# Attention between two scans: the transposes of a query tile one turn later

## The chip, the core and the metric

The kernel runs on one core of a Trainium2 chip. The metric is the time on the device in microseconds (us). TensorE (PE) multiplies and transposes into PSUM, VectorE (DVE), ScalarE (ACT) and GpSimd (POOL) do the elementwise work, SyncE (SP) issues loads. Each engine works through its own list of instructions in the order in which it was written; semaphores tie the lists together. TensorE's clock is granted at one of two levels, 2.4 and 1.2 GHz, which the views show as 1.00 and 0.50.

## What is computed

Two transformer blocks over 1024 tokens of width 1024, one behind the other. The first has a mixing layer of two branches, latent attention and an RWKV recurrence that runs forward and backward, then a convolved feed-forward; the second has gated linear attention, a convolution and a feed-forward. The change touches the first block's attention, which is computed while the two RWKV scans run:

```python
def one_block(args):                        # 128 queries, 8 heads
    qn_b, qr_b = args
    s = (jnp.einsum('bqhd,bkhd->bhqk', qn_b, k_nope)
         + jnp.einsum('bqhd,bkd->bhqk', qr_b, k_rope))
    p = jax.nn.softmax(s.astype(jnp.float32) * scale, axis=-1)
    return jnp.einsum('bhqk,bkhd->bqhd', p.astype(v.dtype), v)
...
def step(state, inp):                       # one RWKV step, both directions
    r_t, w_t, k_t, v_t, a_t, b_t = inp
    sa = jnp.einsum('bhvk,bhk->bhv', state, a_t)
    state = (state * w_t[:, :, None, :] + sa[..., None] * b_t[:, :, None, :]
             + v_t[..., None] * k_t[:, :, None, :])
    return state, jnp.einsum('bhvk,bhk->bhv', state, r_t)
```

## The kernel before

The whole program is written as one list per engine. The stage that matters here is `scans` (line 1894). On every engine it holds four Python generators: `s0` and `s1` are the forward and the backward scan (`scan_pe`, `scan_ve`, `scan_ae`, `scan_ge`, `scan_sp`), `mid` is work between them, and `at_` is the attention. `interleave` (line 163) takes one step of each in the order s0, mid, s1, at_, again and again; one such round is called a turn. After seven turns of s0 alone s1 joins. A scan takes 28 steps for each of 8 chunks of 128 tokens (one step of 225 is the start), and each step is short: matmuls of 64 rows, which ScalarE or VectorE takes out of PSUM, and the scan's next step needs them.

The attention has 64 tiles, each 128 queries by 1024 keys of one head. Its steps for all engines come from one generator, `att_steps` (line 1101), to which each engine gives its own functions:

- `scores(i)`: on TensorE six matmuls of 512 columns into the two banks of `SIDE` (only one tile's scores fit there); on VectorE, as a part of `at_`, the maximum of each row (line 389) and its factor (line 382);
- `later(i)`: on ScalarE the exponential (line 1245), which writes one of two buffers `APB[i % 2]` and releases the score banks;
- `transp(i)`: on VectorE, as `mid` (`att_scale_ve`, line 1214), the reciprocal of the row sum (line 1218) and the scale of the probabilities (line 382, tile `HT`); on TensorE eight 128x128 transposes (line 372) into two banks of the ring `MAIN`, which the scans use too (six banks, taken in order); on ScalarE two copies of 128x512 out of these banks;
- `pv(m)`: on TensorE the product of the values and two tiles' probabilities, on ScalarE a copy, and for every fourth m two stores by GpSimd;
- `load(i)` on SP and `pieces` on ScalarE and GpSimd bring in keys and queries and split them in two parts.

Before the change a tile i has two turns. In the first all engines do `load(i)`, pieces, `scores(i)` and then `transp(i - 1)`; in the second `later(i)` alone, which is nothing on TensorE and VectorE. Behind an odd tile comes a third turn with `pv`. The exponential of tile i reads the maximum of tile i; the scale of tile i-1 reads the exponential of tile i-1; the transposes wait for the scale; the scores of tile i+1 wait for the exponential of tile i, since they take its banks. In a turn, VectorE's order is: step of s0, scale of tile i-1 (`mid`), step of s1, maximum of tile i (`at_`). TensorE's is: step of s0, step of s1, scores of tile i, transposes of tile i-1.

Of the kernel before, what the change touches and what calls it, by code (L numbers as in the profile page):

```python
# [235 lines left out]
def program(nc, a, out):  # L236
    ctx = ExitStack()
    with ctx:
# [862 lines left out]
        def att_steps(scores, transp, pv, load, later=lambda i: None, pieces=lambda *what: None):  # L1101
            load(-1)
            for _ in range(LEAD - 2):
                yield
            for c in range(4):
                pieces("k", 0, c)
            yield
            for c in range(2):
                pieces("q", 0, c)
            yield  # L1110
            for i in range(66):
                if i < 64:
                    load(i)
                    for kind, ahead, c in PIECES[i % 8]:
                        n = (i // 8 if kind == "k" else i // 8 * 2) + ahead
                        if n < (8 if kind == "k" else 16):
                            pieces(kind, n, c)
                    scores(i)
                if 1 <= i <= 64:
                    transp(i - 1)  # L1120
                yield
                if i < 64:
                    later(i)
                    yield
                if i % 2 and i >= 3:
                    pv((i - 3) // 2)
                    yield
# [14 lines left out]
        def att_turns(e):  # L1142
            return att_steps(skip, skip, skip, skip)

        def att_sp(sp):
# [17 lines left out]
            def load(i):  # L1163
# [10 lines left out]
                if i % 8 == 4 and i < 56:  # L1174
                    values(i // 8 + 1)
                    queries(i // 4 + 1)
            return att_steps(skip, skip, skip, load)

        def att_pe(pe):
# [23 lines left out]
            def pv(m):  # L1203
# [4 lines left out]
                for j in range(8):  # L1208
                    for y, cols_ in enumerate(ROWS):
                        x = mm(pe, ps[cols_, b, 0:P], AVH[h % 2][:, j, :], apt(2 * m + y)[:, j * P:(j + 1) * P], j == 0, j == 7)  # L1210
                x.then_inc(*pe.sig("pe_att", "pv", m))
            return att_steps(scores, transp, pv, skip)

        def att_scale_ve(ve):
# [2595 lines left out]
```

How the kernel before makes its waits and increments, by code:

```python
    def wait_ge(self, sem, value):  # L133
        if sem is not None and self.seen.get(id(sem), 0) < value:
            self.seen[id(sem)] = value
            self.e.wait_ge(sem, value)
# [197 lines left out]
        def take(pe, *key, n=1, banks=BANKS):  # L334
            b = plan.next_place(banks, key, n)[1]
            for tok in plan.releases(key):
                pe.wait_ge(*tok)
            return b
# [15 lines left out]
        def load_w(sp, src, *key, n=1024):  # L355
            i = plan.next_place(RING, ("w",) + key)[1]
            for tok in plan.releases(("w",) + key):
                sp.wait_ge(*tok)
            sp.e.dma_start(W[:, 1024 * i:1024 * i + n], src).then_inc(*dma(f"dma_w{i}", *key))
# [58 lines left out]
        def norm1_pe(pe):  # L418
            pe.wait_ge(*at("dma_cst", "all"))
            for t in range(NT + 1):
                if t == NT:
                    project(pe, t - 1)
                    break
                for h in range(2):
                    b = take(pe, "norm1", t, h)
                    pe.wait_ge(*at("ve_norm1", "xs", t))
                    for j in range(4):
                        i = tr(pe, ps[:, b, j * P:(j + 1) * P], TN[t % 2][:, (4 * h + j) * P:(4 * h + j + 1) * P])
                    i.then_inc(*pe.sig("pe_norm1", t, h))
                if t:
                    project(pe, t - 1)
# [1 line left out]
        def project(pe, t):  # L433
# [2 lines left out]
            o, ts_ = ps[:, b, 0:416], slice(t * P, (t + 1) * P)  # L436
            for g in range(2):
                pe.wait_ge(*at("ae_norm1", "hi", t, g))
                pe.wait_ge(*at("ae_norm1", "wm", g))
```

## Time and profile before

| | us |
|---|---|
| median of 3 runs | 3271.42 |
| lowest and highest | 3266.91, 3272.53 |
| the profiled execution | 3270.7 |
| its span, first to last instruction | 3268.9 |
| TensorE matmuls busy, of the span | 3151.0 (96%) |
| VectorE, ScalarE, GpSimd busy | 2089.2, 1296.5, 891.2 |
| mean granted clock of TensorE | 0.989 |

The profile is one execution. Its page names the engines' busy time; the views of the trace behind it show stretches of the span, groups of instructions, waits with what ended them, and instructions in order of time. Times in these views are counted from the first instruction. Weight loads have a row of their own (PEld) and lie beside the matmuls. The ends of matmuls are modelled, so that the next group's start can lie a little ahead of the end shown. A float32 matmul stands as two instructions.

### The profile page before, as it was taken

How to read it: one execution, taken by the hardware profiler on the slowest of the kernel's cores; microseconds unless marked ns; L12 is line 12 of the kernel's file. 1: busy time of each engine (PE TensorE's matmuls, PEld its weight loads, DVE VectorE, ACT ScalarE, POOL GpSimd, SP SyncE). 2: the span in 40 equal slices, each digit the busy share in tenths (PEclk: the TensorE clock that was granted, in tenths of full speed). 3: DMA queues.
4: the chain of work that ended last, by engine and by line, in shares of the span. 5: the costliest groups of instructions: out<-in, count | busy, mean ns of one | idle time of the engine just before them, and what ended most of it. 6: DMA issues, size and time to landing. Idle time of an engine off the chain costs nothing.

```text
span 3268.9 us, 61761 instructions
## 1 busy us (share of the span) xinstructions
PE 3151.0 (96%) x26560; PEld 2539.1 (78%) x26560; DVE 2089.2 (64%) x3031; ACT 1296.5 (40%) x2289; POOL 891.2 (27%) x778
## 2 busy tenths in 40 slices
PE   8989998999999988999999999999999999999998
PEld 8678777788888776467888888878677878888887
DVE  5363465666766665847899887762455475565686
ACT  4333334555555432124333344443333343333444
POOL 1232243232222222100577740000000026666100
PEclk9999999999999999999999999999999999999999
DMA  4251245111211221632132247522102322322753
GB/s 151 68 160 46 71 172 167 41 45 61 71 56 44 79 82 46 214 126 91 71 114 108 97 157 246 167 92 92 39 27 80 130 84 90 116 100 97 265 160 116
DMA packets 128016, 346.46 MB, mean 106 GB/s; under 512 B 15792, under 2 KB 19520, under 8 KB 124928
## 3 DMA queue, kind: packets, MB, share of 16 engines
q1 hardware_dynamic: 106592, 258.09, 24.0%
q0 software_dynamic: 21152, 84.42, 6.9%
q8 instruction: 210, 3.44, 0.5%
q14 instruction: 62, 0.51, 0.1%
HBM read 246.51 MB, written 95.94 MB: 105 GB/s over the span
## 4 chain that ended last, share of the span: by engine, by line
PE 85%; DVE 8%; ACT 4%; issue 2%; DMA 1%; POOL 1%; SPq 0%; DVEq 0%; ACTq 0%; POOLq 0%
PE ps L369 43%; PE ps L368 39%; PE ps L372 4%; DVE AR L378 2%; DVE X L378 2%; DVE SM L389 1%; DVE WS L378 1%; DVE W L378 1%; ACT AR L375 1%; DVE HT L382 1%; ACT WS L375 0%; ACT W L2226 0%; ACT X L375 0%; ACT HT L1245 0%; POOL AR L378 0%
## 5 line engine op out<-in xcount | busy, mean ns | idle before, releaser
L378 DVE TENSOR_TENSOR WS<-W,WS 128x512 fp32r<-128x512 f32 (+1 forms) x284 | 342.1, 1205 | 250.2 <-ACT WS L375 250.0
L368 PE MATMUL ps<-HH,WS 128*128 128x512 f32 x1280 | 394.3, 390 | 0.0
L368 PE MATMUL ps<-TO,WS 128*128 128x512 f32 x1440 | 346.0, 390 | 0.0
L375 ACT ACTIVATE WS<-W 128x512 fp32r<-128x512 f32 (+1 forms) x284 | 210.0, 739 | 315.5 <-PE ps L369 170.8
L368 PEld LDWEIGHTS ps<-TO,WS 128*128 128x128 f32 x1440 | 270.5, 188 | 55.9
L368 PEld LDWEIGHTS ps<-HH,WS 128*128 128x128 f32 x1280 | 240.4, 188 | 49.7
L368 PE MATMUL ps<-HL,WS 128*128 128x512 f32 x640 | 249.3, 390 | 0.0
L368 PE MATMUL ps<-TO 128*128 128x512 f32 x936 | 227.0, 390 | 0.2 <-DVE TO L378 0.2
L369 PE MATMUL ps<-AR 64*64 64x64 f32 (+2 forms) x5440 | 205.2, 244 | 22.3 <-ACT AR L375 11.0
L368 PE MATMUL ps<-WS 128*128 128x512 f32 x888 | 215.2, 390 | 0.1
L375 ACT ACTIVATE X<-ps 128x512 f32<-128x512 f32 (+1 forms) x168 | 100.3, 597 | 285.3 <-PE ps L369 129.1
L369 PE MATMUL ps<-HL,HI 128*128 128x512 f32 (+1 forms) x512 | 207.9, 406 | 2.8 <-POOL WL L378 2.8
L369 PE MATMUL ps<-WS,HH 128*128 128x512 f32 x640 | 203.2, 393 | 4.4 <-DVE X L378 1.5
L369 PE MATMUL ps<-WS,HL 128*128 128x512 f32 x576 | 206.5, 392 | 0.7 <-DVE X L378 0.7
L369 PE MATMUL ps<-HH,WS 128*128 128x512 f32 (+1 forms) x672 | 205.7, 395 | 1.2 <-ACT HH L375 1.2
L369 PE MATMUL ps<-HH,HI 128*128 128x512 f32 (+1 forms) x512 | 204.7, 400 | 0.0
L369 PE MATMUL ps<-HH,WL 128*128 128x512 f32 (+1 forms) x512 | 204.5, 399 | 0.0
L368 PEld LDWEIGHTS ps<-TO 128*128 128x128 f32 x936 | 175.2, 188 | 37.3 <-DVE TO L378 1.3
L369 PEld LDWEIGHTS ps<-AR 64*64 64x64 f32 (+1 forms) x5440 | 158.5, 138 | 56.3 <-issue 27.4
L368 PEld LDWEIGHTS ps<-WS 128*128 128x128 f32 x888 | 166.4, 188 | 34.7 <-DVE WS L378 0.5
L378 POOL TENSOR_TENSOR X<-X 128x1024 f32<-128x1024 f32 (+1 forms) x44 | 104.8, 2385 | 296.3 <-DVE X L378 225.3
L375 ACT ACTIVATE AR<-ps 128x512 f32<-128x512 f32 (+4 forms) x240 | 124.2, 522 | 153.8 <-PE ps L369 105.2
(367 smaller groups left out, 6417.7 us busy)
## 6 DMA issues: line engine op xcount, KB each, us to landing
AR_b<-h_d SPq DMA_DIRECT2D x154, 256.0 KB, 2.9
AR<-rw_d SPq DMA_DIRECT2D x104, 256.0 KB, 4.2
W<-in_w_fg SPq DMA_DIRECT2D x44, 512.0 KB, 3.9
W<-in_w_fu SPq DMA_DIRECT2D x44, 512.0 KB, 5.0
h_d<-FST POOLq DMA_DIRECT2D x20, 1024.0 KB, 4.4
x_d<-X POOLq DMA_DIRECT2D x24, 512.0 KB, 4.6
W<-in_w_tok SPq DMA_DIRECT2D x24, 512.0 KB, 4.4
rw_d<-X POOLq DMA_DIRECT2D x40, 256.0 KB, 3.4
```

What stands on the lines that cost most here:

```text
L368: return pe.e.matmul(o, l, r, start=start, stop=stop, skip_group_check=True)
L369: return pe.e.matmul(o, l, r, start=start, stop=stop)
L372: return pe.e.transpose(o, i, ident)
L375: return e.e.activation(o, x, ACT.Copy)
L378: return e.e.tensor_tensor(o, x, y, op)
L382: return e.e.tensor_scalar(o, x, s1, None, o1)
L389: return e.e.tensor_reduce(o, x, AX.X, op)
```

## The change

In `att_steps` the call of `transp(i - 1)` moves behind `later(i)`, and the `yield` that ends a turn now stands between `scores(i)` and the two. So the first turn of tile i has `load(i)`, pieces and `scores(i)`, the second `later(i)` and then `transp(i - 1)`. Tile 64 and 65, which have no scores, keep one turn each. All engines take the same generator, so the order changes on all of them at once.

```diff
                         if n < (8 if kind == "k" else 16):
                             pieces(kind, n, c)
                     scores(i)
+                    yield
+                if i < 64:
+                    later(i)
                 if 1 <= i <= 64:
                     transp(i - 1)
                 yield
-                if i < 64:
-                    later(i)
-                    yield
                 if i % 2 and i >= 3:
                     pv((i - 3) // 2)
                     yield
```

## Rows read from the trace of the kernel before

**Rows 1.** busy us by stretch: from:to, length, PE, PEld, DVE, ACT, POOL, clock, DMA

```profile
540.00:1124.00 584.00, 550.92 (x11709) 468.15 (x11707) 395.80 (x759) 306.74 (x661) 154.90 (x184) 0.99 0.19 57
1124.00:1290.00 166.00, 144.97 (x4025) 124.01 (x4024) 101.27 (x211) 57.33 (x128) 39.97 (x46) 0.96 0.21 70
1600.00:1700.00 100.00, 100.00 (x443) 82.88 (x442) 93.16 (x76) 39.33 (x67) 68.05 (x43) 1.00 0.29 103
```

**Rows 2.** waits of TensorE's matmuls, 540 to 1124: us, times, longest

```profile
PE ps L372 <- DVE HT L382: 8.7, 9, 2.2
...
PE ps L369 <- ACT HT L1245: 3.5, 4, 2.0
```

**Rows 3.** order of time, TensorE: start, us, engine, line, tiles, shape, count

```profile
807.67 1.65 PE L369 MATMUL ps<-KF,QF 96*128 96x512 f32 x6
809.16 1.04 PE L372 MATMUL ps<-CS,HT 128*128 128x128 f32 x8
810.13 1.08 PE L369 MATMUL ps<-AR 64*64 64x64 f32 x29
...
812.99 0.62 PE L369 MATMUL ps<-EX,AR 64*64 64x64 f32 x13
...
814.25 1.66 PE L369 MATMUL ps<-KF,QF 96*128 96x512 f32 x6
815.75 1.04 PE L372 MATMUL ps<-CS,HT 128*128 128x128 f32 x8
816.72 0.45 PE L369 MATMUL ps<-EX,AR 64*64 64x64 f32 x8
...
819.21 0.45 PE L369 MATMUL ps<-EX,AR 64*64 64x64 f32 x8
...
821.87 1.97 PE L369 MATMUL ps<-W,HT 128*64 128x128 f32 x32
```

**Rows 4.** order of time, VectorE, 809 to 819; brackets: idle before it, releaser

```profile
809.36 1.23 DVE L389 TENSOR_REDUCE SM<-ps 128x1 f32<-128x1024 f32 x1 [3.54 <-PE ps L369]
...
811.33 0.69 DVE L378 TENSOR_TENSOR EX<-ps,AR 128x512 f32<-128x512 f32 x1 [0.55 <-PE ps L369]
...
814.23 0.16 DVE L1218 RECIPROCAL SM<-SM 128x1 f32<-128x1 f32 x1 [0.51 <-ACT HT L1245]
814.43 0.75 DVE L382 TENSOR_SCALAR HT<-HT,SM 128x1024 f32<-128x1024 f32 x1
...
815.95 1.23 DVE L389 TENSOR_REDUCE SM<-ps 128x1 f32<-128x1024 f32 x1
...
817.68 1.51 DVE L378 TENSOR_TENSOR EX<-ps,EX 64x128 f32<-64x128 f32 x4 [0.32 <-PE ps L369]
```

**Rows 5.** waits of the weight loads, 540 to 1124, first and last of 17

```profile
PEld ps L369 <- issue: 40.1, 145, 1.4
...
PEld ps L369 <- DVE X L1644: 0.2, 1, 0.2
```

**Rows 6.** groups by line, 540 to 1124: count, busy us, mean ns, idle

```profile
L389 DVE TENSOR_REDUCE SM<-ps 128x1 f32<-128x1024 f32 x64 | 78.1, 1220 | 27.8 <-PE ps L369 27.1
L1245 ACT ACTIVATE HT<-ps,SM 128x1024 f32<-128x1024 f32 x64 | 71.0, 1110 | 0.0
...
L382 DVE TENSOR_SCALAR HT<-HT,SM 128x1024 f32<-128x1024 f32 x64 | 58.0, 906 | 2.3
...
L382 DVE TENSOR_SCALAR SM<-SM 128x1 f32<-128x1 f32 (+1 forms) x74 | 11.6, 156 | 2.5
```

**Rows 7.** order of time, ScalarE: the two copies of one tile's transposes

```profile
809.80 1.08 ACT L375 ACTIVATE W<-ps 128x512 f32<-128x512 f32 x2 [1.01 <-PE ps L372]
```

**Rows 8.** order of time, TensorE: transposes behind a long wait

```profile
735.69 1.06 PE L372 MATMUL ps<-CS,HT 128*128 128x128 f32 x8 [2.19 <-DVE HT L382]
```

**Rows 9.** busy time before and behind it, columns as in the first group

```profile
730.00:736.60 6.60, 4.41 (x55) 3.60 (x54) 6.06 (x8) 2.11 (x6) 4.23 (x4) 1.00 0.11 40
736.60:740.00 3.40, 3.40 (x56) 3.07 (x56) 2.11 (x4) 1.88 (x5) 0.07 (x1) 0.50 0.02 5
```

## Prediction

> **What bounds the kernel now.** The change touches only the stage in which the two RWKV scans and the attention run in turns, so I read by stage. The busy time of the engines in three stretches [rows 1] comes first: in 540 to 1124 us, where the attention runs, TensorE's matmuls are busy 550.92 of 584 us, VectorE 395.80 and ScalarE 306.74; 33.1 us are TensorE's own idle time, and that is about what there is to win. The waits of TensorE name the pieces of it [rows 2]: transposes that wait for the scaled probabilities (VectorE, line 382) 8.7 us, scores that wait for the exponential which frees their banks 3.5 us; the rest is spread over small waits, most of them of scan steps. In this stage TensorE is the bound, with VectorE next to it.
>
> The order of one turn is what the change turns on, so the third view is the order in time of two tiles, TensorE's instructions [rows 3] and VectorE's [rows 4]. I call the turn with the scores of tile i A, the one behind it B, and the turn with the product by the values, behind every odd tile's B, C. Turn A of tile 30 ends with scores (807.67) and transposes (809.16); B is the stretch 810.13 to 812.99 in which TensorE does scan work alone; A of tile 31 follows with scores at 814.25 and transposes at 815.75, its B from 816.72 to 819.21. VectorE reads in its own fixed order: maximum of tile 30 (809.36) and its scaling by a constant, the first scan's step of B (811.33), the second scan's, then in the next A the reciprocal and the scale of the probabilities (814.23, 814.43), then the next maximum at 815.95, right behind the scores' end.
>
> **The change, part by part.** No instruction is added or taken away and no turn: both orders have 64 A, 64 B, 2 closing A and 32 C turns, 162 in all. Three things move from A(i) to B(i), for 64 tiles: eight transposes on TensorE, the reciprocal and scale of tile i-1 on VectorE, two copies of 128x512 on ScalarE. SP and POOL execute none of the moved steps, and the loads, the pieces and their order against the scans stay; no DMA is issued by a moved step. On ScalarE the exponential of tile i now stands ahead of the copies of tile i-1.
>
> What it removes. The transposes no longer wait in A for a scale that itself waited for the exponential of the turn just before, and the empty turn B, in which a scan step follows the same scan's last one with only one other step between, gets 0.97 us of cover (809.16 to 810.13). The least this gives back is the two waits of attention itself, 8.7 + 3.5 = 12 us [rows 2]. The most is all idle time of the weight loads that has a releaser or none in the table: 17 rows that add up to 81.5 us, of which [rows 5] shows the first and the last. That is far too much, because a load also stands still while the array works on. I take 40 us: the 33.1 us of matmul idle, of which some stays, and some 0.1 us at each of the many waits that a pipelined matmul's modelled end hides.
>
> What it adds: a wait. Today the transposes of tile i-1 are covered twice: VectorE scales before the maximum of tile i is asked for, and TensorE has the scores (1.49 us from start to next start, 807.67 to 809.16) between the scan steps and the transposes. Behind the change VectorE reaches the scale only behind the maximum of tile i, which can't begin before the scores' end, and behind the first scan's step of B; and TensorE has only the two scan steps of B before it wants the transposes. In numbers, from the moment at which TensorE is through with the scores and would start B:
> - maximum and its factor: start 0.1, then 1.22 + 0.156 = 1.38 us [rows 6], so done at about 1.5;
> - the first scan's step on VectorE: the 395.80 us of VectorE less 64 times (1.22 + 0.906 + 2 x 0.156 = 2.44), or 156, leave 240 us for 320 steps (162 turns of one scan, 158 of the other), 0.75 us a step; and it waits for its own inputs, 0.55 us in B(30), 0.32 in B(31) [rows 4], nothing in the turns where that scan has no step for VectorE; I take 0.15 on the mean;
> - reciprocal and scale: 0.156 + 0.906 = 1.06 us [rows 6], and 0.06, an estimate, to the waiting transpose.
>
> That is 3.5 us. TensorE's two scan steps of B took 2.86 us in B(30) and 2.49 in B(31) [rows 3]. Their mean: 584 us less 33 idle, 64 x (1.49 + 0.97) = 157 and 32 x 1.9 = 61 for C's product (a group of 32 matmuls is 1.97 us long in [rows 3], and the next one begins some 0.07 before such an end) leave 333 us in 162 turns, 2.05 us; B turns hold the idle of their own too, so 2.2. The wait is 3.5 - 2.2 = 1.3 on the mean, and 64 of them are 80 us. Two turns by their own rows: B(30): 1.5 + 0.69 + 1.12 = 3.3 against 2.86, a wait of 0.4. B(31): VectorE begins the step at 1.5 instead of 0.96 and is 1.51 long, so 1.5 + 1.5 + 1.1 = 4.1 against 2.49, a wait of 1.6. As bounds for all 64 these give 26 to 102 us. Queued behind the waiting transposes on TensorE is everything, both scans' next steps; behind the scale on VectorE is the second scan's step of B, which TensorE wants only after the transposes (0.97) and one scan step (1.0), so 2.0 us later: it is covered.
>
> On ScalarE turn B now has the exponential, 1.11 us, and two copies, 1.08 us together [rows 6, 7]. The copies follow the transposes, which are late anyway; the next work behind them is the first scan's copy of the next turn, which TensorE needs a further turn later. I cost it at nothing; if the cover is gone it is at most 0.6 us in 64 turns, 38 us, and then the scans wait. The copies also free the two banks of the transposes for the ring of six; same cover.
>
> The clock. In 730.00:736.60 the granted clock is 1.00, TensorE waits 2.19 us for a scale (to 735.69), and from 736.60 the clock is 0.50, the lower level, for 3.4 us [rows 8, 9]. A repeated wait of 1 to 2 us can bring more of these. The stretch behind the attention, 1124 to 1290, is busy to 87% (144.97 of 166) and had 0.96 where the attention's stretch, 94% busy, had 0.99 [rows 1]. With 550.92 busy us in 584 + 40 the stage would be 88% busy; 0.03 less clock is 6% of the time at half rate, which stretches 551 us of work by 3%, 17 us if nothing covers it. Half of such time falls on waits; I take 5 us, bounds 0 and 17. The page "TensorE: Matmul & The Clock Gate" of the Trainium skill (Part 1) says the default state is throttled and activity releases the throttle; the 2.19 us wait and the fall behind it agree.
>
> Sum: +80 for the new wait, -40 for waits given back, +5 for the clock: +45 us. The profiled execution took 3270.7 us, its span 3268.9; it lies within 0.7 us of the median of 3271.4. So 3316 us.
>
> One rule bears on how much idle time there is. The Trainium skill, "Perfetto Trace Analysis", section "Identifying the Most-Contended Engine", says that matmul busy time is a poor measure and that the busy share of LDWEIGHTS is the one to use. By it, with the 82.88% of the stretch 1600 to 1700 as full, the 468.15 us of the attention's stretch are 565 us of full work [rows 1], so that 19 us could be won instead of 40 and the sum would be +66; the two stretches have matmuls of different sizes, so I keep to the matmuls' own idle time.
>
> **Rivals.** (a) The transposes fill the empty turn and their wait stays short: faster. This is what happens if VectorE reaches the scale in time, that is if the mean wait in B is under 40/64 = 0.6 us. For it: B(30) is such a turn, and VectorE is busy only 68% of the stage. Against it: the maximum follows the scores by 0.03 us today (809.32 to 809.36), so it can't come earlier, and no work stands between it and the transposes but two scan steps. With a mean of 0.3 us, 19 us, the time is -40 + 19 = -21: 3250 us. (b) The new wait takes just what it gives back, a mean of 0.6 us, or a larger give-back of 80: 3271 us. (c) The wait as forecast and the clock low for much of the stage, with ScalarE's double load not covered: +80 - 40 + 17 + 25 = +82, 3353 us.
>
> **How the numbers follow.** Forecast 0.62, with 3290 to 3335 of its own (wait 60 to 95, given back 30 to 50); (c) and all beyond 3335: 0.20; (b) 0.07; (a) 0.11. About 0.2% is what a measurement of this kernel can tell from no change. Slower by more holds the forecast and (c): 0.82; same 0.07; faster 0.11. The range goes from 3268, which leaves out (a), to 3360.
>
> **What the profile would show.** Right: the transposes' wait for line 382 grows from 8.7 to some 60 to 90 us and stands at the end of every B; the waits for line 1245 and the scan steps' waits shrink; VectorE runs maximum, one scan step, reciprocal and scale without a gap; the stage ends some 45 us later, at about 1170, and the rest is as long as before. Wrong: the transposes start right behind the second scan's step; or TensorE's scan steps wait for ScalarE's copies behind the exponential; or the granted clock of the stage falls below 0.95, which would put the time over 3335.

## The result and the profile after

The changed kernel takes 3362.1 us (median of 4 runs, 3359.44 to 3365.67) against 3269.64 us before in the same comparison, a ratio of 1.0283 with a 95% interval of 1.0266 to 1.0301. It is 92 us slower. The forecast was slower by 45 us, 3316 us, with a range that ended at 3360: the sign and the main mechanism (a new wait for the scale) held, the size was half of what came, and the time lies 2 us beyond the range.

In the two profiled executions, which differ by 91.8 us, nearly all of it is in the stage that the change touches. Busy time by stretch (from:to, length, then PE, PEld, DVE, ACT, POOL with their counts, granted clock, DMA share, GB/s), first of the kernel before, from its first scores to its last product by the values, and from there to the end:

```profile
538.60:1127.90 589.30, 556.22 (x11792) 472.61 (x11794) 398.84 (x766) 307.60 (x662) 158.32 (x188) 0.99 0.19 57
1127.90:3268.90 2141.00, 2082.11 (x12409) 1661.02 (x12408) 1427.64 (x1924) 794.52 (x1346) 579.59 (x441) 0.99 0.34 117
```

and the same two stretches of the changed kernel:

```profile
541.00:1219.40 678.40, 577.04 (x11792) 482.71 (x11794) 397.15 (x766) 310.57 (x662) 155.48 (x188) 0.96 0.16 50
1219.40:3360.60 2141.20, 2081.83 (x12408) 1659.46 (x12408) 1443.36 (x1924) 793.63 (x1346) 579.05 (x441) 0.99 0.33 117
```

Behind the stage the kernel is as long as before, to 0.2 us, and ahead of it 2.4 us longer (first scores at 541.0 instead of 538.6, in code that the change leaves alone). The stage is 678.4 - 589.3 = 89.1 us longer. TensorE has the same 11792 instructions; its idle time goes from 589.3 - 556.2 = 33.1 to 678.4 - 577.0 = 101.4 us, 68.3 more, and its busy time grows by 20.8 us, while the granted clock of the stretch falls from 0.99 to 0.96. The waits of TensorE's matmuls in the changed kernel (us in total, times, longest) say what the idle time is:

```profile
PE ps L372 <- DVE HT L382: 94.8, 61, 3.3
...
PE ps L369 <- ACT X L1723: 3.4, 3, 1.2
```

The transposes' wait for the scaled probabilities was 8.7 us in 9 places [rows 2] and is 94.8 in 61 now; the scores' wait for the exponential (3.5 us before) is gone from the list, and all waits for ScalarE together are 5.4 us. One tile in order of time, tile 31, whose turn A and B are in [rows 3, 4]. TensorE first, then VectorE:

```profile
849.83 1.66 PE L369 MATMUL ps<-KF,QF 96*128 96x512 f32 x6
851.42 0.45 PE L369 MATMUL ps<-EX,AR 64*64 64x64 f32 x8
...
852.17 1.97 PE L369 MATMUL ps<-X 64*64 64x64 f32 x48
855.38 1.06 PE L372 MATMUL ps<-CS,HT 128*128 128x128 f32 x8 [1.25 <-DVE HT L382]
856.38 0.45 PE L369 MATMUL ps<-EX,AR 64*64 64x64 f32 x8
```

```profile
851.52 1.23 DVE L389 TENSOR_REDUCE SM<-ps 128x1 f32<-128x1024 f32 x1 [0.80 <-PE ps L369]
852.78 0.15 DVE L382 TENSOR_SCALAR SM<-SM 128x1 f32<-128x1 f32 x1
852.86 1.51 DVE L378 TENSOR_TENSOR EX<-ps,EX 64x128 f32<-64x128 f32 x4
854.30 0.14 DVE L1218 RECIPROCAL SM<-SM 128x1 f32<-128x1 f32 x1
854.48 0.75 DVE L382 TENSOR_SCALAR HT<-HT,SM 128x1024 f32<-128x1024 f32 x1
```

TensorE is through with the scores at 851.42 and with both scan steps at about 854.1. VectorE begins the maximum when the scores are done and then works without a gap: maximum, factor, the four instructions of the first scan's step, reciprocal, scale. The transposes start 0.15 us behind the scale, 3.96 us behind the start of the turn. The prediction had put 4.1 us there for this tile. The Trainium skill ("TensorE: Matmul & The Clock Gate", the section on the array's architecture) says that ScalarE and VectorE are strict first-in-first-out; these rows agree.

The clock, columns as in the first view: a stretch in which the transposes wait for a scale, and the one behind it.

```profile
866.00:869.90 3.90, 1.54 (x30) 1.22 (x26) 2.65 (x7) 1.97 (x4) 0.00 (x0) 1.00 0.00 0
869.90:873.30 3.40, 3.40 (x66) 3.28 (x64) 0.57 (x2) 0.71 (x2) 0.00 (x0) 0.51 0.03 5
```

The eight transposes in it waited 2.36 us and began at 868.45; then the clock is at its lower level for 3.4 us. From 546 us to the stage's end there are 14 stretches at the lower level, 55 us together, where the kernel before had two, 10 us. Each of the 14 begins in a wait of TensorE of 1.7 to 3.3 us or at most 1.5 us behind one, and both of the two began so, at waits of 2.2 us. 18 more waits of 1.5 us and over brought no such stretch.

### The profile page after: what moved, and what is told of

It is laid out like the page before. It is cut to its first block, busy times and chain, and to the rows that moved or that the text cites. A ratio compares the mean times of both kernels' runs of the same rounds, so it can differ in the third digit from the quotient of the medians.

```text
span 3360.6 us, 61759 instructions
## 1 busy us (share of the span) xinstructions
PE 3174.1 (94%) x26560; PEld 2547.9 (76%) x26560; DVE 2103.3 (63%) x3031; ACT 1298.6 (39%) x2289; POOL 887.8 (26%) x778
## 4 chain that ended last, share of the span: by engine, by line
PE 83%; DVE 11%; ACT 3%; issue 1%; DMA 1%; POOL 0%; SPq 0%; DVEq 0%; ACTq 0%; POOLq 0%
PE ps L369 41%; PE ps L368 38%; PE ps L372 4%; DVE SM L389 2%; DVE AR L378 2%; DVE HT L382 2%; DVE X L378 1%; DVE W L378 1%; DVE WS L378 1%; DVE EX L378 1%; ACT AR L375 1%; ACT WS L375 0%; ACT W L2226 0%; POOL AR L378 0%; DVE HL L378 0%
## 5 line engine op out<-in xcount | busy, mean ns | idle before, releaser
L378 DVE TENSOR_TENSOR WS<-W,WS 128x512 fp32r<-128x512 f32 (+1 forms) x284 | 351.1, 1237 | 248.2 <-ACT WS L375 248.2
```

What stands on the lines that cost most here:

```text
L378: return e.e.tensor_tensor(o, x, y, op)
```

## The experiments

Times are medians of runs beside the kernel before, ratios are to it. In the diffs the start is the changed kernel, unless said otherwise.

**1. The scale goes back alone.** VectorE's part of the change is undone, TensorE's and ScalarE's stay:

```diff
         def att_scale_ve(ve):
...
-            return att_steps(skip, scale, skip, skip)
+            def ahead(i):
+                if i:
+                    scale(i - 1)
+
+            def last(i):
+                if i == 63:
+                    scale(i)
+            return att_steps(ahead, last, skip, skip)
```

> The changed kernel with one part undone: VectorE scales tile i-1 in the turn of the scores, where it did before the change; TensorE's transposes and ScalarE's copies stay in the turn behind. Theory (VectorE's fixed order makes the wait): the transposes' wait for the scale, 95 us in the changed kernel, falls under 10 us, and what the other waits gave back (18 us of idle time) and the rarer low clock stay, so about 3245 us, faster than before by 0.5 to 1%. Rival (ScalarE's double load in that turn, or the later release of the transposes' banks, holds the scans): the wait moves to the scans' steps and the time stays over 3300 us. Rival (the filled turn is worth nothing): 3270 us.

Measured: 3274.87 us, ratio 1.0020 (1.0012 to 1.0028). All but 6 us of the loss is gone, so the scale's place made it; neither ScalarE's double load nor the transposes' turn did. But the gain that the expectation counted on (3245 us) isn't there: its last rival, a filled turn that is worth nothing, came true. Waits of TensorE's matmuls in this kernel:

```profile
PE ps L369 <- ACT X L1730: 5.4, 3, 2.0
PE ps L369 <- DVE W L378: 5.0, 6, 1.9
PE ps L368 <- issue: 3.3, 2, 2.2
PE ps L369 <- ACT W L375: 2.7, 6, 0.8
PE ps L372 <- ACT AR L1730: 2.5, 2, 1.3
```

and its busy time in the stage:

```profile
542.80:1132.30 589.50, 557.02 (x11792) 464.64 (x11792) 396.29 (x766) 301.81 (x662) 157.66 (x188) 0.99 0.19 57
```

No wait for line 382 or the exponential is left among the large ones, yet TensorE idles 589.5 - 557.0 = 32.5 us, as before (33.1). The same idle time now stands mostly at the scans' own steps, in many small waits.

**2. The scale ahead of the first scan's step** of its turn, still behind the maximum. The order of the generators changes for all engines, but `mid` holds work on VectorE alone:

```diff
-                next(s0)
                 next(mid)
+                next(s0)
                 next(at_)
-            interleave(s0, mid, s1, at_)
+            interleave(mid, s0, s1, at_)
```

> The changed kernel, but VectorE scales tile i-1 ahead of the first scan's step of the same turn instead of behind it. The maximum still stands before it. Theory (the chain maximum, scan step, scale): the chain loses one scan step of 0.75 us and its own wait of about 0.15, so the transposes' wait falls from 1.5 to about 0.6 us a tile, 58 us in all, and with fewer stretches at the lower clock the time is about 3295 us. Rival (the maximum alone decides, or ScalarE does): 3350 us or more.

Measured: 3324.66 us, ratio 1.0170 (1.0153 to 1.0186), 37 us less than the changed kernel's 3362. Of the 94.8 us of the transposes' wait 46.3 are left:

```profile
PE ps L372 <- DVE HT L382: 46.3, 42, 3.1
```

So the scan step is a link of the chain, as held, worth 48.5 us of wait against the 58 expected. But the time fell by less. The stage in this kernel:

```profile
538.60:1176.30 637.70, 562.76 (x11792) 468.94 (x11794) 392.70 (x766) 306.19 (x662) 152.76 (x188) 0.98 0.17 53
```

TensorE idles 637.7 - 562.8 = 74.9 us, 28.6 of it outside that wait, where the changed kernel had 6.6. So 22 of the 48.5 us came back as other waits, most of them at scan steps; that they come from VectorE's steps, now behind the scale, is the likely reason and was not tested by itself. The clock gave 14 us on top (busy time 562.8 instead of 577.0), so the stage is 40.7 us shorter. The expected 3295 left the other waits out.

**3. Work put into the wait.** TensorE gets eight more transposes of the identity a tile, into the bank that the real ones overwrite, ahead of the wait for the scale:

```diff
                     b = take(pe, "pT", i, g, banks=MAIN)
+                    if g == 0:
+                        for j in range(8):
+                            tr(pe, ps[:, b, j % 4 * P:(j % 4 + 1) * P], ident)
                     pe.wait_ge(*at("ve_att", "p", i))
```

> The changed kernel with eight more transposes of the identity (0.97 us, into the bank that the real ones overwrite) ahead of the wait for the scale, on TensorE alone. Theory (TensorE waits 1.5 us a tile there and nothing else is late): 62 us of work fit into the wait, at most 10 us more; and if the lower clock in 54 us of this stage comes from these waits and costs about 20 us, it is gone, so the time is 3345 to 3360 us. Without any part of the clock: 3362 to 3372 us. Rival (TensorE's work is what bounds the stage): 3420 us.

Measured: 3342.06 us, ratio 1.0224 (1.0207 to 1.0242), 3 us under the expected 3345 to 3360: 20 us faster than the changed kernel, with 62 us more work on TensorE. Its stage, and the wait that is left:

```profile
542.90:1204.00 661.10, 618.26 (x12304) 518.90 (x12306) 396.78 (x766) 310.56 (x662) 155.88 (x188) 0.99 0.16 51
```

```profile
PE ps L372 <- DVE HT L382: 34.7, 37, 2.3
```

94.8 - 34.7 = 60 us of the wait took the work in. TensorE's idle time falls by 58.6 us, from 101.4 to 42.8, and its busy time grows by 41.2 instead of 62, so 21 us of the old work's time are gone. The granted clock is back at 0.99 and the stretches at the lower level shrink from 55 to 7 us: 48 us less at half rate are 24 us of work at most. That is what made it faster. So the clock's part in the changed kernel is about 20 us, where the prediction had taken 5 and bounded it by 17.

**4. What the empty turn can hide.** The kernel before, with the same eight transposes in the second turn of each tile:

```diff
+            def fill(i):
+                b = take(pe, "dm", i, banks=MAIN)
+                for j in range(8):
+                    x = tr(pe, ps[:, b, j % 4 * P:(j % 4 + 1) * P], ident)
+                x.then_inc(*pe.sig("pe_dm", i, frees=("dm", i)))
-            return att_steps(scores, transp, pv, skip)
+            return att_steps(scores, transp, pv, skip, later=fill)
```

> The kernel before with eight more transposes of the identity (0.97 us) in the second turn of each tile, in which TensorE has no attention work, 62 us in all. It measures what the empty turn can hide. If the empty turn hides what the waits of the scans behind it gave back in the changed kernel (about 18 to 27 us), the time is 3305 to 3315 us. As the prediction had it (40 us): 3292 us. If the turn is empty time in full: 3270 us. If it hides nothing: 3332 us.

Measured: 3313.32 us, ratio 1.0137 (1.0121 to 1.0153). 62 us of work cost 45, as expected (3305 to 3315), so the empty turn hides 17 us and not 40. Its stage, in which TensorE idles 19.0 us instead of 33.1:

```profile
538.60:1169.60 631.00, 612.02 (x12304) 523.48 (x12304) 402.34 (x766) 311.00 (x662) 157.88 (x188) 0.99 0.17 54
```

**5 and 6. A shorter maximum**, over 512 instead of 1024 scores (what is computed is another softmax), in the changed kernel and in the kernel before:

```diff
-                red(ve, m, ps[:, b:b + 2, :].rearrange("p a b -> p (a b)"), ALU.max).then_inc(*ve.sig("ve_att", "max", i))
+                red(ve, m, ps[:, b + 1, :], ALU.max).then_inc(*ve.sig("ve_att", "max", i))
...
-                ts(ve, nb, m, -SCALE, None, ALU.mult, None).then_inc(*ve.sig("ve_att", "nmax", i))
+                ts(ve, nb, m, -SCALE / 16, None, ALU.mult, None).then_inc(*ve.sig("ve_att", "nmax", i))
...
-                                bias=sm(264 + i % 4, 1), scale=SCALE,
+                                bias=sm(264 + i % 4, 1), scale=SCALE / 16,
```

> The changed kernel with the maximum over 512 instead of 1024 scores of each row (and a flatter exponential, so that nothing overflows): what is computed is another softmax, the instructions and their sizes are otherwise the same. The maximum falls from 1.22 to about 0.69 us. Theory (the maximum stands at the head of the chain that the transposes wait for): each tile gains 0.53 us, 34 us in all, and some of the low clock goes with it, so 3362 - 34 - 5 to 10 = 3320 us. Rival (only the scan step and the scale bind): no change, 3360 us.

> The same shorter maximum (another softmax) in the kernel before. Theory: there the transposes cover the maximum, and the same 0.53 us a tile is worth little, 0 to 8 us, so 3262 to 3270 us. Rival (VectorE bounds both orders alike): 30 us less, 3240 us.

Measured: the maximum takes 0.69 us instead of 1.22, and the changed kernel 3333.39 us, ratio 1.0197 (1.0183 to 1.0211), 29 us less; the kernel before 3267.92 us, ratio 0.9998 (0.9989 to 1.0007), nothing. The same instruction costs in one order and not in the other: in front of the scale it is on the path, under the transposes it isn't. The transposes' wait in the changed kernel with the short maximum:

```profile
PE ps L372 <- DVE HT L382: 74.0, 54, 3.2
```

It fell by 21 us, not 34, and the time is 13 us over the expected 3320: in some turns the scan's step behind the maximum waits for its own inputs anyway. VectorE's idle time between the maximum and that step grows from 6 to 16 us over the stage.

**7. The same short maximum in the kernel of experiment 1.**

> The same shorter maximum (another softmax) in the kernel with VectorE's scale back in the turn of the scores (3274.87 us). It tells why filling the empty turn gained nothing there. If it is because the maximum, with no transposes behind the scores any more, now delays the scans' VectorE steps of the next turn: 15 to 30 us less, 3245 to 3260 us. If the scans' own chains or ScalarE are the cause: under 6 us less, 3269 us or more.

Measured: 3265.84 us, ratio 0.9989 (0.9980 to 0.9998), 9 us less than 3274.87. That lies between the two expectations (under 6 and 15 to 30). VectorE's maximum is a part of why nothing was gained there, but a small part; that it costs because no transposes stand behind the scores any more to cover it is argued.

**8. Longer copies on ScalarE, in the kernel of experiment 1.** Its two copies of a tile cut in eight, in the turn that also has the exponential:

```diff
-                    cp(ae, apt(i)[:, 512 * g:512 * g + 512], ps[:, bank("pT", i, g), :]).then_inc(
+                    for j in range(3):
+                        cp(ae, apt(i)[:, 512 * g + P * j:512 * g + P * j + P], ps[:, bank("pT", i, g), P * j:P * j + P]).then_inc(
+                            *ae.sig("ae_att", "part", i, g, j))
+                    cp(ae, apt(i)[:, 512 * g + 384:512 * g + 512], ps[:, bank("pT", i, g), 384:512]).then_inc(
```

> The kernel with VectorE's scale back in the turn of the scores, and ScalarE's two copies of a tile's transposes cut in eight of 128x128 (0.28 us each), which makes the copies about 1.1 us longer in each turn that also has the exponential; the result is the same. If ScalarE's double load in that turn bounds the order: 40 to 70 us more, 3315 to 3345 us. If it has room there: under 10 us more, 3285 us at most.

Measured: 3275.89 us, ratio 1.0026 (1.0016 to 1.0036), 1 us more. But the edit loaded ScalarE by less than was expected of it. The copies of one tile, in experiment 1 and here:

```profile
855.15 1.08 ACT L375 ACTIVATE W<-ps 128x512 f32<-128x512 f32 x2
858.70 1.45 ACT L375 ACTIVATE W<-ps 128x128 f32<-128x128 f32 x8
```

The eight copies take 0.31 us each but overlap, so a tile's copies take 0.37 us longer and not 1.1, 24 us in 64 tiles. The expectation's 40 to 70 us stood for three times that load, so this run shows room for 0.37 us a turn and no more. The stronger evidence is elsewhere: experiment 1 has the exponential and both copies in one turn and a stage as long as before, and in the changed kernel TensorE waits for ScalarE 5.4 us in all. The prediction had costed it at nothing.

**9 and 10. Two other orders on VectorE**, both with the transposes in their new turn. In 9 the scale stands right ahead of the maximum, behind both scan steps of the first turn:

```diff
         def att_ve(ve):
+            scale = att_scale_ve(ve)
...
             def scores(i):
+                if i:
+                    scale(i - 1)
                 m, nb = sm(256 + i % 4, 1), sm(264 + i % 4, 1)
```

In 10, from the kernel of experiment 1, the maximum moves as `later` of `mid` behind the first scan's step of the second turn:

```diff
-            return att_steps(ahead, last, skip, skip)
+            return att_steps(ahead, last, skip, skip, later=top)
...
-            return att_steps(scores, skip, skip, skip)
+            return att_steps(skip, skip, skip, skip)
```

where `top(i)` is the maximum and its factor, word for word.

> The changed kernel with VectorE's scale of tile i-1 at the end of the turn of the scores, right ahead of the maximum of tile i, so that both of the scans' steps go before it; transposes and copies stay in the turn behind. Theory (the scale is what the transposes lack, and any place before the maximum is early enough): the transposes' wait stays under 10 us; VectorE scales while TensorE multiplies the scores, and the scans' steps are no longer held by it, so 3255 to 3272 us. Rival (scale and maximum in a row are late and hold the scans' next steps): 3280 us or more.

> The kernel with the early scale (3274.87 us) with the maximum of tile i moved too, into the turn behind, after the first scan's step. The short maximum took 9 us off this order, so VectorE's maximum holds scan steps. If that is its place in the list, 5 to 10 us less, 3265 to 3270 us. If instead the later exponential now holds the next scores (they take its banks), a wait of scores on line 1245's successor of over 20 us, and 3290 us or more.

Measured: 3289.76 us, ratio 1.0063 (1.0050 to 1.0075), and 3299.69 us, ratio 1.0095 (1.0079 to 1.0111). Both expectations for my theory were missed. In 9 the transposes' wait is short, 11.4 us in 10 places against 8.7 in 9 in the kernel before, a little over the 10 us expected, so the scale is early enough:

```profile
PE ps L372 <- DVE HT L382: 11.4, 10, 3.1
```

But TensorE idles 610 - 562.4 = 47.6 us in 540 to 1150:

```profile
540.00:1150.00 610.00, 562.41 (x11932) 469.64 (x11934) 404.70 (x770) 304.08 (x667) 159.22 (x190) 0.99 0.18 55
```

The other waits are small and many, most of them at scan steps. That the scans wait for VectorE's two long instructions in a row is argued, not shown, and the order has a second cost: the 64 scales take 65.9 us of VectorE instead of the 57.7 in experiment 1, because more of them are long ones (the last section has these). In 10 the scores wait only 6.1 us for the exponential (the rival had asked for 20). The stage is 28.8 us longer than in experiment 1: 6.1 of it is this wait, 12.6 are other waits, most of them at scan steps, and 10.1 are TensorE's busy time at a granted clock of 0.97:

```profile
PE ps L369 <- ACT X L1738: 8.7, 3, 3.3
PE ps L369 <- ACT W L375: 7.8, 8, 2.2
PE ps L369 <- DVE W L378: 7.3, 5, 1.9
PE ps L369 <- ACT HT L1260: 6.1, 5, 3.2
```

Each place on VectorE holds something else; no place that I tried beats the kernel before.

**11. The scale behind the maximum, transposes where they were.** The kernel before, with VectorE's scale at the end of its turn:

```diff
         def att_ve(ve):
...
-            return att_steps(scores, skip, skip, skip)
+            return att_steps(scores, att_scale_ve(ve), skip, skip)
```

(`att_scale_ve` then returns its function `scale`, and `mid` is empty.)

> The kernel before with one thing changed: VectorE scales tile i-1 behind the maximum of tile i, at the end of the same turn. TensorE's order is as before, its transposes right behind the scores. Theory (what costs is the scale's place behind the maximum on VectorE, not the transposes' new turn): each tile's transposes wait for 1.38 + 1.06 + 0.1 us behind the scores, less nothing, 2.5 us x 64 = 160 us, less 20 to 30 given back, plus some 30 of low clock: 3410 to 3440 us. Rival (the loss of the changed kernel comes from the transposes' turn): 3270 to 3290 us.

Measured: 3513.77 us, ratio 1.0740 (1.0722 to 1.0758), 244 us slower, and 74 us beyond the expected 3410 to 3440. The transposes' wait and the stage:

```profile
PE ps L372 <- DVE HT L382: 165.9, 63, 5.5
```

```profile
544.30:1372.80 828.50, 645.11 (x11792) 541.36 (x11792) 398.12 (x766) 313.12 (x662) 153.08 (x188) 0.87 0.13 41
```

The wait is what the chain says, 160 expected and 165.9 found, with TensorE's order untouched: it is VectorE's order that makes the loss. What I had too low is the clock: 0.87 in the stage, 218 us of it at the lower level, which at half rate can cost 109 us (the same instructions are busy 89 us longer than before), where I had put 30.

**12. Both gaps.** The kernel of experiment 1 with the eight transposes of the identity behind the scores, where the real ones stood:

```diff
                 x.then_inc(*pe.sig("pe_att", "sc", i))
+                b = take(pe, "dm", i, banks=MAIN)
+                for j in range(8):
+                    x = tr(pe, ps[:, b, j % 4 * P:(j % 4 + 1) * P], ident)
+                x.then_inc(*pe.sig("pe_dm", i, frees=("dm", i)))
```

> The kernel with the early scale (3274.87 us) and eight more transposes of the identity (0.97 us a tile, 62 us in all) right behind the scores, where the real transposes stood before the change. It asks why filling the empty turn gained nothing: whether the place behind the scores, now empty, opened as large a gap (VectorE's maximum and the scans' steps behind it) as the one that was filled. If so, this order is that of the kernel before with its empty turn filled (3313 us): 3303 to 3320 us, the extra work costs 62 less some 17 to 25 us. If the gaps come from the scans' own chains, wherever TensorE's attention work stands: 3330 us or more.

Measured: 3312.23 us, ratio 1.0131 (1.0114 to 1.0148), 37 us more than experiment 1 for 62 us of work; 25 us are hidden there. It is the time of experiment 4 (3313.32), as expected. With work in both places it doesn't matter which is the real one, and with work in one place only, the other has about as much idle time to hide work in (17 us there, 25 here). That is why experiment 1 gained nothing.

## Why the prediction was right or wrong

**The mechanism of the loss** was right: the chain scores, maximum, one scan step, scale, transposes, with only two scan steps of TensorE beside it. Experiments 1, 2, 5 and 11 each change one link or its place, and the transposes' wait follows (from 94.8 us to none among the large ones, 46.3, 74.0, and 165.9); experiment 6 shortens a link where it isn't on the path, and nothing changes. All three terms of the sum were sized too favourably, and one of them, the waits given back, was also wrong in kind.

**The new wait**, put at 1.3 us a tile and 80 us, measured 94.8. The chain's length was right: over 63 tiles the transposes start on the mean 3.55 us behind the start of their turn, where the sum had 3.5. The other side was off: I took TensorE's scan steps as 2.2 us, raised from the 2.05 worked out because the turns "hold the idle of their own too". Once TensorE waits in nearly every turn, that idle time is in the wait: the steps took 2.05 us, so 1.5 us is left. The 2.05 should have stood. (64 times 1.3 is also 83 and not 80.)

**The waits given back**, put at 40 us, measured 26.5: the old wait of the transposes, 8.7, and 17.8 of the others (24.4 idle before without it, 101.4 - 94.8 = 6.6 after). This is the step that failed in kind: filling the empty turn was taken as a gain by itself. I took all of the matmuls' idle time, 33.1, and added a hidden tail. Experiment 4 shows that the empty turn hides 17 us, and experiment 1 that this is no gain either: without the new wait TensorE idles 32.5 us, as before, since the place that the transposes leave has as large a gap. What went away in the changed kernel are waits that lie inside the new one. The estimate of 19 us, which the prediction worked out from the rule of the Trainium skill on LDWEIGHTS ("Perfetto Trace Analysis", "Identifying the Most-Contended Engine"), was nearer than my 40 and gave the nearer sum, +66.

**The clock**, put at 5 us with bounds 0 and 17, measured about 20: 20.8 us more busy time in the same instructions, and 20 us back in experiment 3. The fall itself, 0.99 to 0.96, is the one that the prediction had read from the stretch behind the attention. What failed is its price. Of the time at the lower level I had said that half falls on waits, and taken 5 of 17; measured, little of it does: TensorE's matmuls are busy in 52 of the 59 us at the lower level in the whole stage. And the 17 was 3% of the 551 busy us, where the time at the lower level is a share of the whole stage with its waits: 3% of 678 us is 20.

The three together: 94.8 - 26.5 + 20.8 = 89.1 us, which is the stage's growth; the forecast's were 80 - 40 + 5. All three missed the same way, by 15, 13.5 and 16 us, and that put the time beyond the range.

**The rivals.** (a), faster, and (b), no change, needed a mean wait of 0.6 us or less (or, for (b), 80 us given back); it is 1.5. (c), 3353 us, came nearest, but 25 us of it are for ScalarE, whose double load experiment 1 shows to cost next to nothing. Its clock term, 17 us, was nearly right. The signs of being right held: the wait of line 382 in nearly every B (61 places), and 2141 us behind the stage; "60 to 90 us" and "about 1170" were too little. One sign of being wrong did not work: a clock below 0.95 was to go with a time over 3335 us, and the time passed that with the clock at 0.96.

## What to carry to other kernels

Moving an engine's work into its own idle slot moves the matching work on every engine that shares the schedule: look at what then stands ahead of it in the list of the engine that feeds it, and what it used to cover where it stood. An idle slot in a ring of dependent steps (here each scan step needs the one before) isn't free time: filling it left as large a gap at the place the work came from. And if a change adds a short wait to each of many turns, price the lower clock behind it with the same care as the wait.

## What the runs showed of the hardware

A kernel became 20 us faster by 512 useless transposes (experiment 3): with waits of 1.7 to 3.3 us between dense work TensorE's clock fell to its lower level 14 times in the stage, and with work in them it fell twice, 0.96 against 0.99. The Trainium skill ("TensorE: Matmul & The Clock Gate", Part 1) has the default throttled and activity releasing it; the runs agree, and in experiment 11, with 165.9 us of such waits, the stage's clock is 0.87.

The scale on VectorE takes 0.75 us as a rule and at times much longer. In the kernel before:

```profile
842.99 3.51 DVE L382 TENSOR_SCALAR HT<-HT,SM 128x1024 f32<-128x1024 f32 x1
```

while GpSimd ran

```profile
843.16 2.11 POOL L378 TENSOR_TENSOR AR<-AR,CS 128x256 f32<-128x256 f32 x3
845.24 0.71 POOL L378 TENSOR_TENSOR QF<-AR,QF 96x256 fp32r<-96x256 f32 x1
```

The Trainium skill ("Perfetto Trace Analysis", "Optimizing Scalar/DVE Operations") says that GpSimd and VectorE share a read port of SBUF, and that an operation of VectorE which uses two ports holds it as a lock. In this case's traces the two go together. Of the 896 scales in the 14 traces, 587 have no TENSOR_TENSOR of GpSimd beside them, and none of these takes over 0.76 us. All 157 that take 0.9 us or more have one beside them, and each lasts as long as the stretch shared with it, or up to 0.8 us longer; the other 152 have one beside them and stay under 0.9 us. So the cost of the same scale goes with its place in time against GpSimd's work: 57.7 us for the 64 scales in experiment 1, 65.9 in experiment 9. This fits a VectorE that waits for GpSimd, though the scale's row begins 0.17 us ahead of GpSimd's here; no run took the one away to see the other, so the cause stays open.
